# Two attention layers of a transformer kernel: scores one step ahead, transposes in banks of their own, later high parts, fewer and larger table loads

## The reference

```python
# nsa_attention, 16 heads of 64 in 4 key groups; o_cmp, o_sel, o_win share q
k_cmp = compress(kvh(kc), pe_k, w1_k, w2_k)          # gelu(blk @ w1) @ w2, blocks of 32 keys, stride 16
p_cmp = masked_softmax(q . k_cmp * scale + bias_c)   # 15 block keys
o_sel = softmax attention on the selected blocks of 64 keys, with rel_bias
o_win = banded attention, 0 <= distance <= 255, with rel_bias
o = g[..., 0:1] * o_cmp + g[..., 1:2] * o_sel + g[..., 2:3] * o_win

# dilated_attention, three groups (window, dilation) = (128,1), (512,4), (2048,16)
q = (h @ w_q).reshape(B, S, 3, N_KV, GQA_R, HEAD_DIM)
for each group: keys t, t-d, ..., t-window;  o_gi, lse_gi
alpha = softmax(lse over the three groups);  o = sum_gi alpha_gi * o_gi
```

## Time and profile before

| | us |
|---|---|
| median of 3 runs | 1891.92 (1890.75 to 1892.8) |
| the profiled execution | 1888.3 |
| its span, first to last instruction | 1886.5 |
| mean granted clock of TensorE | 0.967 of 2.4 GHz |

### The profile page before, as it was taken

How to read it: one execution, slowest core, us unless ns; L and a number is a source line. 1 busy time by engine, 2 the same in 40 slices (tenths; PEclk the granted TensorE clock), 3 DMA queues, 4 the chain that set the end, 5 groups by cost and what they waited for, 6 DMA issues and landing times.

```text
span 1886.5 us, 31683 instructions
## 1 busy us (share of the span) xinstructions
PE 1794.1 (95%) x13416; PEld 1684.9 (89%) x13416; DVE 1222.6 (65%) x1918; ACT 935.6 (50%) x1280; POOL 124.1 (7%) x35
## 2 busy tenths in 40 slices
PE   7999999999999999999999978799999988889998
PEld 6999999999889999999998877569998977779996
DVE  6976766877569767668775657556554734456453
ACT  5446565544355465655443546445443654445442
POOL 2612000000017120000000000000000000000000
PEclk9899999999999999999999999789999998899999
DMA  8684445555546644455555462224555645225552
GB/s 235 163 235 147 149 157 186 167 183 179 202 140 188 192 144 148 157 191 166 180 179 205 135 181 91 90 67 157 179 201 194 182 139 134 90 90 184 185 211 79
DMA packets 249148, 305.75 MB, mean 162 GB/s; under 512 B 9778, under 2 KB 224142, under 8 KB 249007
## 3 DMA queue, kind: packets, MB, share of 16 engines
q1 hardware_dynamic: 235959, 289.66, 47.7%
q10 hardware_dynamic: 13048, 14.07, 3.5%
HBM read 299.51 MB, written 4.19 MB: 161 GB/s over the span
## 4 chain that ended last, share of the span: by engine, by line
PE 76%; DVE 10%; DMA 6%; ACT 5%; issue 2%; DVEq 1%; ACTq 0%; SPq 0%
PE psum L463 23%; PE psum L464 23%; PE psum L465 23%; DVE wlo L439 3%; DMA raw<-in_b_w_q 2%; ACT whi L431 2%; DMA raw<-in_w_ffn_gate 2%; PE psum L2385 1%; DMA raw<-in_a_w_in 1%; DMA raw<-in_b_w_out 1%; ACT work L2018 1%; DVE work L2246 1%; DMA x<-in_x 1%; DMA raw<-in_a_w_out 1%; DVE hT L617 0%
## 5 line engine op out<-in xcount | busy, mean ns | idle before, releaser
L431 ACT ACTIVATE whi<-raw 128x2048 fp32r<-128x2048 f32 (+2 forms) x277 | 526.6, 1903 | 552.3 <-PE psum L465 177.6
L439 DVE TENSOR_TENSOR wlo<-raw,whi 128x2048 fp32r<-128x2048 f32 x249 | 563.3, 2281 | 183.3 <-PE psum L465 158.7
L463 PE MATMUL psum<-hT,whi 128*128 128x256 f32 x2160 | 616.9, 286 | 7.5 <-DVE wlo L439 3.8
L464 PE MATMUL psum<-hT,whi 128*128 128x256 f32 x2160 | 613.0, 284 | 0.0
L465 PE MATMUL psum<-hT,wlo 128*128 128x256 f32 x2160 | 612.9, 284 | 0.0
L463 PEld LDWEIGHTS psum<-hT,whi 128*128 128x128 f32 x2160 | 416.4, 193 | 10.9 <-issue 5.5
L464 PEld LDWEIGHTS psum<-hT,whi 128*128 128x128 f32 x2160 | 416.5, 193 | 0.1
L465 PEld LDWEIGHTS psum<-hT,wlo 128*128 128x128 f32 x2160 | 416.2, 193 | 0.0
L439 POOL TENSOR_TENSOR wlo<-raw,whi 128x2048 fp32r<-128x2048 f32 (+1 forms) x28 | 122.8, 4390 | 585.6 <-ACT whi L431 402.7
L463 PE MATMUL psum<-whi,hT 128*128 128x256 f32 (+2 forms) x448 | 145.1, 324 | 1.1 <-issue 1.1
L465 PE MATMUL psum<-whi,hT 128*128 128x256 f32 (+2 forms) x448 | 144.3, 322 | 0.0
(11 more groups left out here) (352 smaller groups left out, 2832.0 us busy)
## 6 DMA issues: line engine op xcount, KB each, us to landing
raw<-in_w_in SPq DMA_DIRECT2D x78, 1024.0 KB, 5.7
raw<-in_ffn_w_up SPq DMA_DIRECT2D x44, 1024.0 KB, 5.2
raw<-in_w_ffn_gate SPq DMA_DIRECT2D x22, 1024.0 KB, 5.4
raw<-in_w_ffn_up SPq DMA_DIRECT2D x22, 1024.0 KB, 6.4
raw<-in_w_ffn_down SPq DMA_DIRECT2D x22, 1024.0 KB, 5.0
raw<-in_ffn_w_down SPq DMA_DIRECT2D x22, 1024.0 KB, 5.2
raw<-in_b_w_q SPq DMA_DIRECT2D x12, 1024.0 KB, 5.7
raw<-in_a_w_in SPq DMA_DIRECT2D x10, 1024.0 KB, 5.8
```

The costliest lines, as they stand in the source:

```text
L431: act.activation(part(whi, n, HIGH_SLOTS), part(raw, n, RAW_SLOTS), ACT.Copy).then_inc(high_made, 1)
L439: eng.tensor_tensor(part(wlo, n, LOW_SLOTS), part(raw, n, RAW_SLOTS), part(whi, n, HIGH_SLOTS).bitcast(F32), ALU.subtract).then_inc(stream ...
L463: nc.tensor.matmul(dst, left[0], right[0], start=first, stop=False)
L464: nc.tensor.matmul(dst, left[0], right[1], start=False, stop=False)
```

## The change

In both layers:

- `scores(s + 1)` is issued in step s, before `context(s - 1)` and `turn(s)`, and waits for the maxima of step s instead of the copies. `turn(s)` writes to banks of its own: 6 and 7 in the compressed layer. In the dilated layer blocks of four (t = 1) or three (t = 0) go to banks 1, 5, 7 or 5, 7. Probabilities and statistics have two buffers.
- DVE's order is `weigh(s)`, `maxima(s + 1)`, then the step's other work. ACT's is `exps(s)`, `copies(s - 1)`, then the rest, with the high parts mostly last. The last but one eviction of the lead carries no high part; the last one makes two.

In the compressed layer the contexts use banks 4 and 5 for two groups each: for groups 0 and 1 ACT copies them to SBUF (`take_group`, steps 8 and 9), `block_context` writes to a bank of its own, and DVE adds (`sum_group`). The halves of `FILL` come earlier, `block_scores` is split over steps 11 and 12, `block_weights` over 13 and 14, the memset of `cprob` moves to step 11, and a small Exp in the lead loads the exp table. `block_high(1)` waits for `block_low(0)`.

In the dilated layer query units from 9 on use bank 4 alone, six halves a quad stand in four places, DVE copies each pair's context to SBUF (`take_context`), and lows run one unit further ahead. Tables of the dilated layer lie in `band_dram` by head, and a quad loads in four DMAs after the other work of its step.

```diff
-                        act.dma_start(table_dram[i, :, :, 0:SPAN], spread(tab[0:QH, i, :], 1, ROWS)) \
+                        home = band_dram[:, i - 1] if i else table_dram
+                        act.dma_start(home[:, :, 0:SPAN], spread(tab[0:QH, i, :], 1, ROWS)) \
...
-            TURN_HIDDEN, KEY_OUT, VALUE_OUT, CMP_SCORES, CMP_TURN = (13, 14), 15, 16, (17, 18), (19, 20)
-            products = 21
-            FILL = {0: ((6, 0), (6, 1)), 1: ((7, 0), None), 2: ((7, 1), (8, 0)), 3: ((8, 1), None), 4: ((9, 0), None),
-                    5: ((9, 1), (10, 0)), 6: ((11, 0), None), 7: ((12, 0), (13, 0)), 8: ((14, 0), None), 9: ((14, 1), None)}
+            TURN_HIDDEN, KEY_OUT, CMP_SCORES, VALUE_OUT, CMP_TURN = (13, 14), 15, (16, 17), 18, (19, 20)
+            GROUP_BLOCKS = (21, 22)
+            products = 23
+            FILL = {0: ((6, 0), (6, 1)), 1: ((7, 0), (7, 1)), 2: ((8, 0), (8, 1)), 3: ((9, 0), None), 4: ((9, 1), None),
+                    5: ((10, 0), None), 6: ((11, 0), None), 7: ((12, 0), None), 8: ((13, 0), None), 9: ((14, 0), (14, 1))}
...
                 def scores(s):
                     j, t, keys = step(s)
                     if s:
-                        pe.wait_ge(turned_copied.sem, turned_copied.at(2 * s))
+                        pe.wait_ge(maxima_ready.sem, maxima_ready.at(2 * s))
...
                         pe.wait_ge(probs_ready.sem, probs_ready.at(2 * s + e + 1))
+                        if s:
+                            pe.wait_ge(turned_copied.sem, turned_copied.at(2 * s + e - 1))
                         for n in range(2 * (t + 1)):
-                            mm = nc.tensor.transpose(slot(e)[:, n * P:(n + 1) * P], probs_s[:, e, n * P:(n + 1) * P], ident)
+                            mm = nc.tensor.transpose(bank(6 + e)[:, n * P:(n + 1) * P],
+                                                     probs_s(s)[:, e, n * P:(n + 1) * P], ident)
...
+                scores(0)
                 for s in range(STEPS):
-                    scores(s)
                     fill(s, 0)
+                    if s + 1 < STEPS:
+                        scores(s + 1)
...
+                def take_group(g):
+                    act.wait_ge(group_ready.sem, group_ready.at(g + 1))
+                    act.wait_ge(bank_full.sem, bank_full.at(product_of[11] + 1))
+                    act.activation(part[:, g, :], bank(4 + g), ACT.Copy).then_inc(group_taken.sem, 1)
+
                 def block_high(i):
                     act.wait_ge(blocks_ready.sem, blocks_ready.at(i + 1))
+                    if i:
+                        act.wait_ge(operand_ready.sem, operand_ready.at(i))
...
+                def sum_group(g):
+                    p = GROUP_BLOCKS[g]
+                    dve.wait_ge(bank_full.sem, bank_full.at(p + 1))
+                    dve.wait_ge(group_taken.sem, group_taken.at(g + 1))
+                    dve.tensor_tensor(part[:, g, :], own(p), part[:, g, :], ALU.add).then_inc(group_summed.sem, 1)
```

The dilated layer:

```diff
+            FILL = {}
+            for g in range(QUADS - 1):
+                a, b, c = ([(LEAD + ND * g + i, j) for j in range(2)] for i in range(ND))
+                FILL[4 * g - 1], FILL[4 * g] = (None, None, a[0]), (a[1], None, b[0])
+                FILL[4 * g + 1], FILL[4 * g + 2] = (b[1], None, c[0]), (None, c[1], None)
...
+            def turn_bank(s, i):
+                return bank(((5, 7), (1, 5, 7))[step(s)[1]][i])
+
             def own(n):
-                return bank(4 + n % 2)
+                return bank(4 + n % 2) if n < LEAD else bank(4)
...
-                            pe.wait_ge(bank_free.sem, bank_free.at(n - 1))
+                            pe.wait_ge(bank_free.sem, bank_free.at(n if n >= LEAD else n - 1))
...
                     if s:
-                        pe.wait_ge(turned_copied.sem, turned_copied.at(2 * s))
+                        pe.wait_ge(maxima_ready.sem, maxima_ready.at(2 * s))
                     if s % 4 == 0:
                         pe.wait_ge(bank_free.sem, bank_free.at(LEAD + ND * (j // 2)))
                     for st in range(ND):
+                        if t and s and st == 2:
+                            pe.wait_ge(turned_copied.sem, turned_copied.at(turns_until(s - 2) + 1))
...
                 for s in range(STEPS):
-                    scores(s)
-                    if i < 2 * count:
-                        dense_half(i)
-                        i += 1
+                    fill(s, 0)
+                    if s + 1 < STEPS:
+                        scores(s + 1)
+                    fill(s, 1)
                     if s:
                         context(s - 1)
                     turn(s)
-                    if s % 2 == 0 and i < 2 * count:
-                        dense_half(i)
-                        i += 1
+                    fill(s, 2)
...
+                    exps(s)
+                    if u < count and i == 3:
+                        evict(u + 2)
+                    if s:
+                        copies(s - 1)
+                    if u < count and i < 2:
+                        evict(u + i)
+                    if s >= 4 and s % 2 == 0:
+                        high(s // 2 - 2)
+                    if u < count and i != 2:
+                        make_high(act, n0 + u + (0, 1, None, 2)[i] + HIGH_SLOTS + 1)
                     if i == 0 and hq < QUADS - 1:
                         tables(hq + 1)
...
+                make_lows(dve, n0 + LEAD + 2)
+                maxima(0)
                 for s in range(STEPS):
...
+                    weigh(s)
+                    if s + 1 < STEPS:
+                        maxima(s + 1)
                     if s and s % 2 == 0:
-                        low(s // 2 - 1)
+                        take_context(s // 2 - 1)
                     if s % 4 < 3:
-                        make_lows(dve, n0 + min(LEAD + ND * (s // 4) + s % 4 + 2, count + 2))
+                        make_lows(dve, n0 + min(LEAD + ND * (s // 4) + s % 4 + 3, count + 2))
+                    if s >= 4 and s % 2 == 0:
+                        low(s // 2 - 2)
```

357 lines of the change are left out of this document (211 added, 146 removed).

## The result

The changed kernel takes **1812.1 us** (median of four runs, 1811.3 to 1818.2) against 1892.4 us for the kernel before, measured beside it (1890.8 to 1893.8): ratio 0.9583, 95% interval 0.9561 to 0.9605. Measured again on two more chips the ratio is 0.9617 (0.9586 to 0.9649) and 0.9619 (0.9594 to 0.9643). The forecast was 1833 us with a range from 1815; it had the direction and the place, and was too slow by 21 us against the first median and by 16 and 14 against the other two (1817.3 and 1818.6). The profiled execution took 1818.2 us, its span is 1816.4.

What follows compares the result with a forecast made beforehand. TensorE, busy 95% of the span, was taken as the bound, losing time to idling and low clock in two attention loops. Gains of 36.4 (dilated) and 23.1 us (compressed), 59.5 together, gave 1833 us, range 1815 to 1857.

Steps and rivals of the forecast that it cites:

- the sum of PE's work: Dilated loop: eight pairs of steps and 18 dense halves take 106.4 us of TensorE at 2.4 GHz, against 149.9.
- 0.6 + 3 for the chain at the end: Dilated loop: last four steps, without halves, cycle in 7.0 us a pair against 6.7 of PE; 0.6 + 3 added.
- The 3.5 us for one fall of the clock: Dilated loop: the clock falls once, costing half a pair of steps, 3.5 us.
- The tables' issues: Dilated loop: bias table issues held ACT 6.01 us ahead of exps; four larger ones behind other work, taken as 3.
- the forecast's 1108.4 and 1109.9: Compressed loop's start: exps(0), behind high parts 8 and 9 and a DMA, at 1108.4; first weighting's first half near 1109.9.
- The 98.4 us from the first weighting to the last: Compressed loop: VectorE binds, its work plus 3.5 of gaps and exp waits giving 98.4 us between these points.
- The allowances of 9 + 3 + 2 us: Compressed loop: 9 for a tail at 1.2 GHz, 3 for a clock fall at exps(0), 2 for `block_high(1)` waiting.
- Rival (1): The clock stays up in both layers' tails since PE has shorter gaps: minus 9, 3 and 3.5, 1817 us; chance 0.15.
- (2): Last dilated quad: transposes don't hold the clock, which stays at 1.2 GHz; 8 us more, 1841; chance 0.10.
- (3): Both loops: the pipeline forms only by half, the wait for weights is only shortened; 1860 us; chance 0.15.
- (4): Both loops: fine interleaving of short matmuls and waits keeps TensorE at 1.2 GHz; slower, about 1995 us; chance 0.03.
- (5): Whole kernel: no change, because the weights' stream sets the pace; chance 0.02.

Runs made afterwards that it cites:

- serial_copies: The changed kernel with scores(s + 1) behind the transposes of step s and copies(s - 1) ahead of exps(s) again, in both layers: 1865.5 us, ratio 0.9888.
- ahead_copies: The changed kernel with only ScalarE's order put back, copies(s - 1) ahead of exps(s), in both layers; TensorE's look-ahead stays: 1829.4 us, ratio 0.9688.
- dve_less: The changed kernel without 28 of the 32 additions of position terms in the compressed layer's blocks of keys and values on VectorE: 1817.2 us, ratio 0.9624.
- tails_serial: The changed kernel with scores 13, 14 and 15 behind the transposes of the step before, in both layers; earlier steps keep the look-ahead: 1845.4 us, ratio 0.9745.
- after_again: The changed kernel, unedited, run again on another chip for a second profile: 1817.3 us, ratio 0.9617.
- ahead_off: The changed kernel with scores(s + 1) issued behind the transposes of step s in both layers; ScalarE's new order stays: 1892.1 us, ratio 0.9996.
- pool_lows: The changed kernel with four low parts of the compressed layer's weights made by GpSimd, not VectorE: 1826.7 us, ratio 0.9678.

## Why the prediction was right or wrong

**Right: where and why.** The losses named, PE's waits for the weighting and for the copies, and the low clock in each loop, are what shrank, and `serial_copies` and `ahead_copies` show that the look-ahead is behind most of it in the compressed layer and part of it in the dilated one. Forecast were 59.5 us of gain, measured about 74 in the two layers.

**Dilated, the sum of PE's work: right.** 106.4 us forecast at full clock, 105.7 measured; 0.6 + 3 for the chain at the end against 4.4 us of idle. **The 3.5 us for one fall of the clock: wrong**, it was 1.00 throughout, and this is the whole difference (loop 110.1 against 113.5). ScalarE and VectorE do keep up, as worked out. The tables' issues did matter, as the term had it: put back, they cost 5 us.

**Compressed, the start: the time nearly right, the reason right, a second wait missed.** The stage of this profile began 3.6 us later than that of before (1064.3 against 1060.7), so the forecast's 1108.4 and 1109.9 are 1112.0 and 1113.5 in its time. exps(0) ran at 1110.50, and the first weighting's half was done at 1112.6: 1.5 and 0.9 early. I had them wait for high part 9 and its DMA, and in all three profiles of the changed kernel exps(0) stand directly behind that high part, which had waited 0.4, 2.3 and 2.8 us for its DMA. But the maximum that exps(0) need was ready only 0.5 to 0.9 us earlier: it had waited 6.9 us and more for the loads of w2. I had counted their issues (as a delay of `evict(3)`), not that VectorE's wait counts their landing.

**The 98.4 us from the first weighting to the last: the number right, the bound doubtful.** The last weighting ended at 1211.25, 98.6 us after 1112.6; in the other two profiles it is 100.1 us. But `dve_less` took 5.3 us from VectorE, and this stretch is still 97.9 us, so VectorE does not bind it as a whole. I had worked with one sum over the whole loop. That the early steps have TensorE's halves as the longer side would explain it, but is not shown. That the sum came out within 0.2 us of the first profile is luck in part, and no proof of it.

**The allowances of 9 + 3 + 2 us: the step that failed.** They stood for a tail at the low clock, a fall at exps(0) and a wait of `block_high(1)`. Behind the last weighting (1211.25) came 8.2 us, where the sum has 4.4 and these 14. Stage start to loop end was to be 166.0 us (1226.7 less 1060.7) and was 155.2 to 156.9: 9 to 11 too long. I had taken the clock of the last 27 us of before as a property of the work there (no dense halves, 0.50 though PE was busy in 21.6 of 27). It went with how TensorE's work was issued: with the look-ahead the last 27.3 us of the compressed loop are at 0.82 and the last 23.7 of the dilated one at 1.00. Rival (1) had it, for the dilated tail wholly and for the compressed one mostly. `tails_serial` shows the cause by taking the look-ahead out of the last steps, which brings gaps of 3.4 to 3.8 us and the low clock back. Rival (1)'s reason, shorter gaps, is not shown as such, since the clock of before was low with gaps under 2.3 us. The "against" that I set beside rival (1) came from rows that the change was about to alter. The 3 us at exps(0) are the least wrong of these terms: the first profile has no time at 1.2 GHz there, the other two have 3.4 and 6.8 us.

**The remainder.** Both mis-sized clock terms are 3.5 + 9 to 11, 13 to 14 us too long. That takes 1833 to 1819 to 1820, and the repeated medians are 1817.3 and 1818.6. The profiles agree with this: 1828.8 less 13 to 14 is 1815 to 1816 for an execution without the gap at 118 to 142 us, and `after_again`, which has none, took 1814.1. The first median, 1812.1, lies another 5 to 6 us below the repeated ones. That is as much as this gap is worth, and three of those four executions left no trace, so the cause stays open. I had made one sum against one profile and given this scatter no term; the range's lower end at 1815, 2 us under rival (1)'s 1817, had no room for it. Small slips made no difference: 1828.8 and 3.6 are 1832.4, not 1833, and the terms of the last steps' cycle add to 6.8 us, not 7.0.

**The other rivals.** (2) fell with the clock of 1.00 in the last quad. (3) did not come: the waits for the weighting are 8.0 and 0 us. (4) did not come as written, but `ahead_off` shows the neighbouring danger: with ScalarE's new order and without TensorE's all the gain is gone. (5) is excluded by the change of 80 us at the same bytes.

**What was to be seen in the profile.** Dilated loop 110 to 118, PE idle under 8: 110.1 and 4.4. Compressed 120 to 130: 112.9, too short. DVE over 75%: 83% (93.88 of 112.90). Waits of the transposes under 8: 8.0, just missed, and none. Clock of at least 0.93 in the dilated loop: 1.00. Near 0.5 in the last 25 us of the compressed one: wrong, 0.82. exps(0) behind a high part: yes. ACT's high parts no longer waiting for b_w_q: wrong, the line below is the changed kernel's dilated loop; but with 4.4 us of idle in that loop little of it can have reached TensorE.

```profile
ACT whi L435 <- DMA raw<-in_b_w_q: 10.0, 2, 5.2
```

## What to carry to other kernels

When a change shortens TensorE's gaps, the clock that a stretch had before is no price for it afterwards: here these terms were 13 us of a 21 us miss. Neither the total of idle time nor the longest gap would have told the new clock, so give such a term a range that includes nothing, and test it with a variant that changes the gaps alone. Look-ahead on one engine has to be matched by the order on the engine that serves it, and a semaphore shared by an urgent and a late load makes both urgent. Set the sum against several executions, as untouched stretches ahead of the loops can shift one profile by up to 8 us against the next.

## What the runs showed of the hardware

A two-element operation of VectorE took 4.29 and 4.42 us instead of 0.16 while GpSimd worked on 128x2048 elements (`pool_lows`); an idle GpSimd is no free helper for a loop with many small SBUF-to-SBUF operations on VectorE. The granted clock stayed at 1.00 over 126.5 us with 18.1 us of idle time in gaps up to 2.37 us (`serial_copies`), fell at gaps of 3.4 to 3.8 us (`tails_serial`), and also in the kernel before, where the last dilated steps have gaps of at most 2.27 us and 27 us of the compressed ones are at 0.50 with gaps of at most 1.99. So no single length of gap tells it. Issues of DMAs on ScalarE's queue are not of one price: the four table loads behind an idle queue took 0.31, 0.73 and 1.91 us for the last two, and the w2 load behind them 5.17 us, though it is smaller.
